# A two-block network on one core: the second recurrence's score products with two halves of stationary columns, and its keys, values and removal keys turned in two row halves

## The reference

```
def _rwkv7_step(S, inp):
    r, w, k, v, kk, b = inp
    sa = jnp.einsum('bhvk,bhk->bhv', S, kk)
    S = S * w[:, :, None, :] - sa[..., None] * b[:, :, None, :] + v[..., None] * k[:, :, None, :]
    return S, jnp.einsum('bhvk,bhk->bhv', S, r)
```

## Time and profile before

| | |
|---|---|
| median of three runs | 4652.1 us |
| the profiled execution | 4639.85 us |
| its span, first to last instruction | 4638.1 us |
| mean granted TensorE clock | 0.976 of full speed |
| TensorE, VectorE, ScalarE, GpSimd busy | 93%, 56%, 31%, 20% |
| instructions profiled | 98,695 |

### The profile page before, as it was taken

The page is one execution under the profiler, slowest core; times in us unless marked ns, Lnnn a source line. Parts: engine busy times, 40 slices in busy tenths (PEclk is TensorE's granted clock), DMA queues, the critical chain, the costliest instruction groups (busy, mean ns, idle before and its releaser), DMA issues. The chain is left out here.

```text
span 4638.1 us, 98695 instructions
## 1 busy us (share of the span) xinstructions
PE 4306.3 (93%) x42610; PEld 2633.3 (57%) x42610; DVE 2605.2 (56%) x4158; ACT 1445.0 (31%) x2274; POOL 949.7 (20%) x1027
## 2 busy tenths in 40 slices
PE   9998989899999999999899988999999879989898
PEld 4445955444444445555688855664444368866673
DVE  5753466786442225775444456567587634446556
ACT  3212353100000112332233355544233223336552
POOL 0002311000110000000233243540000033324460
PEclk9998999999999999999899999999999999999999
DMA  4332021343433543444422111312344432211222
GB/s 137 110 90 83 2 92 64 127 136 127 139 133 123 183 143 127 158 142 156 132 65 65 38 47 46 99 55 86 128 169 156 140 118 59 65 42 44 70 60 84
DMA packets 341470, 468.80 MB, mean 101 GB/s; under 512 B 39559, under 2 KB 244647, under 8 KB 340080
## 3 DMA queue, kind: packets, MB, share of 16 engines
q1 hardware_dynamic: 289216, 266.26, 18.6%
q0 software_dynamic: 51824, 196.24, 12.2%
HBM read 328.14 MB, written 147.86 MB: 103 GB/s over the span
## 5 line engine op out<-in xcount | busy, mean ns | idle before, releaser
L491 PE MATMUL psum<-arena 128*128 128x512 f32 x2352 | 1034.8, 596 | 17.6 <-POOLq L222 7.2
L491 PEld LDWEIGHTS psum<-arena 128*128 128x128 f32 x2352 | 446.8, 191 | 566.4 <-issue 547.5
L3299 PE MATMUL psum<-arena 64*64 64x64 f32 (+4 forms) x24624 | 689.9, 231 | 82.7 <-issue 51.4
L3299 PEld LDWEIGHTS psum<-arena 64*64 64x64 f32 (+2 forms) x24624 | 635.1, 140 | 138.3 <-issue 78.1
L1079 PE MATMUL psum<-arena 128*128 128x512 f32 x1344 | 582.3, 594 | 12.3 <-DVEq L222 5.3
L706 PE MATMUL psum<-arena 128*128 128x512 f32 x1232 | 535.8, 595 | 4.4 <-DVE arena L772 2.5
L2677 DVE CUSTOM_DVE_ANT_0 arena<-psum,arena 128x512 f32<-128x512 f32 (+3 forms) x532 | 292.6, 588 | 296.7 <-PE psum L2564 291.4
L1079 PEld LDWEIGHTS psum<-arena 128*128 128x128 f32 x1344 | 254.1, 190 | 330.8 <-issue 318.6
L706 PEld LDWEIGHTS psum<-arena 128*128 128x128 f32 x1232 | 232.3, 190 | 301.3 <-issue 291.7
L2564 PE MATMUL psum<-arena 64*128 64x512 f32 (+3 forms) x1192 | 273.1, 543 | 86.6 <-DVE arena L2677 69.4
L2642 ACT COPY arena<-psum 128x512 f32<-128x512 f32 (+3 forms) x532 | 244.8, 512 | 303.5 <-PE psum L2615 297.6
(11 more groups left out here) (348 smaller groups left out, 5167.9 us busy)
## 6 DMA issues: line engine op xcount, KB each, us to landing
arena<-w_in SPq DMA_DIRECT2D x86, 512.0 KB, 5.7
proj<-arena SPq DMA_DIRECT2D x172, 256.0 KB, 2.0
arena<-w_mod POOLq DMA_DIRECT2D x24, 1024.0 KB, 5.7
arena<-down_sum SPq DMA_DIRECT2D x40, 512.0 KB, 3.7
arena<-proj POOLq DMA_DIRECT2D x31, 640.0 KB, 5.0
arena<-proj SPq DMA_DIRECT2D x28, 640.0 KB, 7.2
arena<-w_down SPq DMA_DIRECT2D x30, 512.0 KB, 3.9
x_home<-arena POOLq DMA_DIRECT2D x26, 512.0 KB, 5.2
```

What stands on the lines that cost most here:

```text
L491: ins = pe.matmul(ps[:, b, :], L[:, k, :], R[:, k, :], start=(p in ("P1", "P5", "P6", "P7") and k == 0), stop=(k == KT // 2 - 1), skip_gro ...
L3299: return pe.matmul(out, lhsT, rhs, start=first, stop=last, skip_group_check=not (first and last))
```

## The change

In `scores` each product of 64 rows, 128 stationary and 128 moving columns is made by two matmuls with 64 stationary columns each. The inner order over `c` and `p` goes round the four quadrants of the array: output partitions `HALF[c ^ p]`, input partitions `HALF[p]`. In `turn` each transpose of a 128 x 128 tile becomes two of 64 partitions x 128 columns, one for each head; the result is laid out by head p and then by pair i, where it had been by direction d and then by tile. `val`, through which H, G and O read the turned tiles, follows that layout.

```
-        val = lambda x, d, p, j: self.part(f"t{x}", d)[:, j * P + 64 * p:j * P + 64 * p + 64]
+        val = lambda x, d, p, j: self.part(f"t{x}", p)[:, (RT * d + j) * 64:(RT * d + j) * 64 + 64]
...
             for j in range(RT):
-                for p in range(2):
-                    ins = mm(out[:, p, j * P:(j + 1) * P], head(l, d, p, j, n), head(r, d, p, j, n))
+                for c in range(2):
+                    for p in range(2):
+                        ins = mm(out[HALF[c ^ p], p, j * P:(j + 1) * P], head(l, d, p, j, n)[:, HALF[c ^ p]], head(r, d, p, j, n))
...
             out = start(f"t{x}@{n}")
-            for d in range(2):
-                for j in range(RT):
-                    ins = pe.transpose(out[:, d, j * P:(j + 1) * P], b[f"{x}{d}{n % 2}"][:, j * P:(j + 1) * P], ident)
+            for i, (d, j) in enumerate(pairs):
+                for p in range(2):
+                    ins = pe.transpose(out[:, p, 64 * i:64 * i + 64], head(x, d, p, j, n), ident[HALF[p], HALF[p]])
             ins.then_inc(s.sem, 1)
```

## The result

The changed kernel takes 4687.8 us (median of four runs, 4683.6 to 4693.5) against 4650.9 us: ratio 1.008, 95% interval 1.0062 to 1.0097. It is 37 us slower (29 to 45 by the interval). The profiled execution took 4693.5 us with a span of 4691.7, 53.6 us more than before.

What follows compares the result with a forecast made beforehand. TensorE was taken as the bound, its two stages held by instruction fetch. First half 1.85 us more, second 1.1 less: 0.75 a chunk, 15 over 20 chunks, profiled 4655; timed runs 12 above, so 4668 us; range 4618 to 4702.

Steps and rivals of the forecast that it cites:

- Bound and mechanism: TensorE in both stages: stands still at ends of 256-instruction packets until the next arrives; 3.6 us a block, 353 packets after.
- Rival 1: Both stages: fetch stays as hidden as now, gaps do not grow; 4618 us, or 4642 with the lower saving; chance 0.22.
- rival 2: Each chunk: cover stays at 1.95 us, first half +0.7, second -1.1 to -0.7; about 4652 us; chance 0.22.
- Execution of the scores: Six score steps of a chunk: four quadrants take turns without loss, 0.9 us less a chunk (0.5 to 1.9).
- Rival 4: Score steps: four quadrants moving 128 columns do not overlap beyond two; +48 us, 4700; chance 0.08 together with rival 3.
- Execution of the turns: Turns of each chunk: 36 half transposes overlapping in two row halves, 0.8 us less a chunk (nothing to 1.1).
- the sum: Over 20 chunks: 34 us less execution if nothing else were asked; with the fetch, 0.75 us a chunk, 15 us more.
- First half of a chunk: From the end of the turns, 1491 instructions, 5.82 blocks at the fetch's pace: 21.4 us, 1.85 more.
- Second half: O through the next turns: O untouched at 4.5 us, then 4.22 blocks at the fetch's pace; 18.9 us, 1.1 less.
- 0.8 us of cover: Start of each half: time covered by a block fetched during slower work in front, 0.8 us, against 1.95 before the turns.
- rival 3: Each chunk: blocks cost the present average of 3.95 us, +2.7 us a chunk, 4706 us; chance 0.08 together with rival 4.
- the likeliest case: Whole kernel: the forecast itself, slower through instruction fetch, 4668 us, own range 4661 to 4700; chance 0.48.

Runs made afterwards that it cites:

- the run with less execution: Changed kernel with 64 moving columns in place of 128 in all six score steps, same instruction list: ratio 1.0083 against the kernel before.
- the shift of 176 instructions: Kernel before with 44 matmuls (176 instructions) of the first A of each layer done twice: ratio 1.0050, 23 us slower.
- QK alone: Kernel before with only the two QK score steps split; RK, RB and the turns as before: ratio 1.0038, 18 us slower.
- the turns alone: Kernel before with only the turns split, with the layout of their result, scores as before: ratio 1.0011, 5 us slower.
- the doubled x2: Kernel before with 12 of the 24 matmuls of x2, in each chunk's dense half, done twice: ratio 1.0047, 22 us slower.

## Why the prediction was right, and where it was short

- *Bound and mechanism.* Right. Rival 1 (the fetch stays hidden) fell by "issue", 119.0 us, and by the run with less execution; rival 2 (it cancels, 4644 to 4660) by the time. 354 packets came for the 353 forecast. One reading was loose: 1.45 us is the longest gap of that chunk, not of the stage (2.3).
- *Execution of the scores.* Right by the stretch of a step: RK0 and RK1 take 1.30 us for 48 recorded matmuls, 0.027 us each, against 1.53 (the row's count of 58 has matmuls of neighbouring steps that were in flight). Rival 4 fell with it. The sign that the prediction named was another, the group's busy time per matmul, 0.028 (wrong if 0.05), and that came out at 0.045:

```profile
L3299 PE MATMUL psum<-arena 64*64 64x128 f32 x3120 | 140.6, 273 | 16.0 <-issue 13.9 <-ACT arena L3507 1.8
```

  The group also holds O's 432 matmuls, which took 30.9 us before, and counts each run of matmuls until its last one has landed (273 ns in flight). Without O's it is 0.041. The sign was ill chosen; the stretch is what a step costs.
- *Execution of the turns.* Right where nothing interrupts them: 1.26 us for a stretch that took 2.11; 1.3 was forecast. In 7 of the 20 chunks they take 1.75 to 1.79, most often with a wait for VectorE's L3556 that the kernel before does not have there; the mean is 1.45, so 0.66 us less a chunk for the 0.8 forecast. The total, 20 us less on the page, is below the 34 of the sum: L3299's 64*64 64x64 form, which did not change, is busy 442.5 us for 429.2. That gaps cut its runs apart, so that more of them are counted to their last landing, would explain it, but is not shown.
- *First half of a chunk.* 21.98 us, forecast 21.4, before 19.55. Over 14 chunks it grew by 2.4 us for the 1.85 forecast.
- *Second half.* 20.33 us, forecast 18.9, before 20.00; over 14 chunks it grew by 0.2 us, where 1.1 less was forecast. This is the term that was mis-sized, in sign too. I priced its 4.22 blocks behind O at 3.6 us each; two blocks there with a gap at either end took 3.82 and 3.86, and the median of the 105 such blocks in both stages of the changed kernel is 3.84. And I let each half start with 0.8 us of cover. The whole comes to 2.76 us in this chunk, 2.5 on the average (44 us over 18 chunks), for 0.75.
- *A price nearer to the stages* stood in my own reading: one packet per 4.1 us in the whole stage. 13.3 blocks by 4.06 us are 54 us; the two stages as a whole, from L3299's first instruction to its last, grew from 805.5 us (2253.0 to 2662.3 and 3734.3 to 4130.5) to 853.3 (2255.4 to 2685.5 and 3760.8 to 4184.0), 48 us. The timed runs lost 37, so this price is too high for them by as much as the forecast's was too low: 4688 lies halfway between rival 3's working (every block at the average, 4706), which had little chance, and the forecast of 4668.
- *What I left out:* that a chunk of nearly ten whole blocks may be a good case that another length gives up, as the shift of 176 instructions suggests. QK alone fits but does not show it: 3.75 blocks by 3.85 us are 14 us, and 18 were lost (11 to 25 by the interval).
- *Sign and range.* Slower by over 0.2% had 0.54 of the chance; 4687.8 is within 4618 to 4702 and within the likeliest case's own 4661 to 4700. The sign came from the mechanism. The size did not: the sum said 15 us more and 37 came, and the width of the range carried it.

Still open: why 1.2 us pass before the packet is seen and 2.5 us after it with the DMA engines nearly idle (share 0.01 to 0.02 in the blocks of 3.82 and 3.84 us), and whether fewer or later loads would shorten the one of 4.6 to 4.9 us. Neither was tried.

## What to carry to other kernels

Where TensorE's matmuls are so small that 256 of its instructions run in less than some 4 us, count instructions before counting matmul time: here the two stages took 4.11 us for each packet before (196 in 805.5 us) and 4.08 after (209 in 853.3), and 21 us less matmul work in them made them 4 us shorter. As a price for a single change it is rough: 2.8 blocks for the turns alone would be 11 us and 5 were lost, 3.75 for the doubled x2 would be 15 and 22 were lost. Gaps called "issue" whose distances are multiples of 127 or 128 matmuls are the mark of it. Splitting a matmul into quadrants did not pay here; that it would where the list has room, and that fewer and larger matmuls would help where the fetch is the bound, follows from the argument but was not run. A difference of 0.2 to 0.5% between two such kernels may be no more than a shift of the block ends.

## What the runs showed of the hardware

- The instructions of TensorE came in packets of 16.4 KB, 256 instructions. In the blocks with a gap at either end the packet was seen 1.2 us (median) after the block before had begun, and TensorE resumed 2.5 us after it. Such blocks took 3.84 us (median), 4.58 and 4.85 us while loads of keys and values held the DMA engines at a share of 0.94 to 0.97. The Trainium skill, "Runtime: NRT & Kernel Launch", section "Instruction fetch mechanics", calls the crossing of a block mostly hidden; for these stages the measurements decide against it.
- Four quadrants of 64 x 64 moving 128 columns took 0.027 us per matmul (48 in 1.30 us), 0.11 us for the four; two quadrants took 0.125 us for a pair. No idle time stood between them and the 64 x 64 steps at their ends in that stretch.
- In the 64*128 form, moving 64 columns took nearly as long as moving 128 (0.073 and 0.076 us per matmul).
